# Forget sums of the sampled requests: gathered by key, summed on chip, added to the scores by a product with the unit matrix

## The chip, the cores and the metric

The program runs on one core of one Trainium2 chip. The metric is the device time of one execution in microseconds (us), from the first to the last work of the core. The core has TensorE (PE, with weight loads shown as PEld), VectorE (DVE), ScalarE (ACT), GpSimd (POOL) and SyncE (SP), which here does nothing but issue DMAs. All data is fp32 unless bf16 is named.

## The reference

Two decoder layers handle one new sequence of 1024 positions and, with the same weights, eight sampled requests of eight new tokens each, whose 2048 past positions lie in pages of 128. One of four mixers is attention with forget gates (FoX). For a request it computes:

```
suf  = reversed cumsum of past_logf  -  past_logf      # per head: the sum over all later past positions
lnew = cumsum(logf)                                    # over the eight new tokens
fk   = concat([-suf, lnew])
score[t, key] = q[t] . k[key]  +  lnew[t] - fk[key]    # masked beyond the token, then softmax
```

So each score of a past key gets two terms: `suf` of its key (2048 keys, 4 heads, 8 requests) and `lnew` of its query row. The page table says in which pages of the cache the request's keys and log forget values lie.

## The kernel before

**Stages of a layer.** The first stage normalises, makes the GLU product and then, tile by tile, the input projections; beside it POOL gathers the NSA cache in 16 pieces of 1 MB (`raw_in`, line 2377) and the sampled requests' compressed keys are made. A barrier (`everyone`, `arrive`) ends it. The attention stage follows (about 474 to 1000 us in layer 0, 2454 to 2985 in layer 1), then merge and the feed-forward products (`gemm`, line 884), which the change does not touch.

**The attention stage.** Its order is written out by hand: 96 units `u` (4 heads, 8 tiles of queries, 3 kinds). Per unit PE makes the scores of unit u+2 (`scores`, line 1220), transposes the probabilities of unit u (line 1253), then does the extras of the unit, then the values of u-1 (`values`, line 1239). DVE takes the row maximum (`row_max`, line 1973), ACT the exponential (line 1489). The work of the eight requests is cut into extras (`extras_of`, `request_steps`): request b begins at unit 7 + 10 b. `kt` transposes its keys (line 1121), `ds` makes its scores (line 1128 for the FoX keys, s below 4, with strips of 32 columns; line 1138 for the NSA keys), `pt` transposes its probabilities, `pv` makes its values. All extras and the transposes of the probabilities share two PSUM banks in turn: `open_group` waits until DVE or ACT has emptied the group before last. In FoX `ds`, DVE adds the tile BIAS to the scores as it copies them out and takes their maximum (`scored`, line 2071).

**How BIAS comes about.** At the start of the attention stage POOL gathers the log forget values, one page a partition (LFP, line 2404). DVE scans each head (line 1914) and copies the totals; PE multiplies them by a triangular mask that adds the totals of later pages (line 1196); DVE makes `suf` (`later_sums`, line 1926, suf_ready). SP stores it to suf_s in eight DMAs (line 696), copies it within DRAM into bias_s, once per new token (line 699, 2 MB), and loads it for each request (`bias_in`, line 717). The terms of new keys go by new_s (line 679) and sixteen copies (line 692); the query terms come into FQ by sixteen small loads (line 688). POOL adds FQ and a mask to BIAS (lines 2429 and 2431, bias_add).

**Queues.** SP's queue in the attention stage, in order: KV4, `head_in(0)` (lines 669 to 672: QN, QF, KF, VF of a head), GH, new_s, the q_in loads (680 to 683), GB and FQ, the copies to bias_s, the stores of suf_s, the copy of line 699, `sparse_in(0)` (sixteen page loads at line 707, each with the page number read from a table, and four more), `bias_in(0)`, two outputs, `head_in(1)`, then per unit: at unit 9 the rank exchange (lines 738 to 746), at unit 12 + 10 b `bias_in(b+1)`, at unit 7 + 10 b `sparse_in(b)` after `pv` of the request before, and at units 27, 51, 75 the head's output and a further head load. POOL's queue: the forget gather, four memsets (line 2408), a wait for suf_out, the gather `fox_in(1)` (line 2393, 4.2 MB: keys and values of request 1 into KVP[1]; LFP, PFX and SUF lie in the same memory), then BIAS by request, with `fox_in(b)` after `pv(b-2)`. `fox_in(0)` is issued at the end of the first stage. DVE's queue: the scans, the copies of ten groups `kv` and `q`, `later_sums`, `row_max(0)`, `row_max(1)`, then unit by unit. PE starts `q` transposes (line 1022) when all four loads of `head_in(0)` have landed.

Of the kernel before, what the change touches and what calls it, by code (L numbers as in the profile page):

```python
# [46 lines left out]
SUFW = PAST // 4 + NT  # L47
# [12 lines left out]
def shape_constants():  # L60
# [26 lines left out]
    parts["later"] = ((q // NPG == k // NPG) & (q > k))  # L87
# [60 lines left out]
def build_step(nc, A, O, layers=DEPTH, stop=99):  # L148
    ctx = ExitStack()
    with ctx, nc.allow_non_contiguous_dma(reason="columns of a few elements in small tables"):  # L150
# [18 lines left out]
        suf_s = scratch("suf_s", (NB, 4 * NH, PAST // 4))  # L169
        bias_s = scratch("bias_s", (NB * 4 * NH, NT, SUFW))  # L170
        new_s = scratch("new_s", (NH, NB, NT))
# [19 lines left out]
        page_rows = fixed.take(1).bitcast(I32)  # L191
# [13 lines left out]
        t1 = Layout(arena, glu_at, ARENA_W)  # L205
        Z = t1.take(1164)
# [69 lines left out]
        FQ = lo.take(NB)  # L276
        GB = lo.take(NB * 3, b=NB, c=3)
        BIAS = lo.take(SUFW)
# [6 lines left out]
        KNT = lo.take(4 * NS, g=4, n=NS)  # L285

        lo = Layout(arena, lo_end, ARENA_W - 544)
        WNP = lo.take(4 * P, j=4, n=P)
        SF = lo.take(SUFW)
        SSL = lo.take(SUFW)  # L290
# [7 lines left out]
        OO = lo.take(GW, h=NH, d=HD)  # L298
# [6 lines left out]
        l2 = Layout(arena, late_at - (P + NT) - SUFW, late_at)  # L305
# [28 lines left out]
        l2 = Layout(arena, kp_at, kp_at + NPG * 512)  # L334
        LFP = l2.take(PAGE * NH, t=PAGE, h=NH)
        PFX = l2.take(NH * PAGE, h=NH, t=PAGE)
        SUF = LFP.rearrange("p t h -> p (t h)").rearrange("p (g s q) -> p g s q", g=4 * NH, s=4)
        TOT = l2.take(4)
        LAT = l2.take(4)
# [79 lines left out]
        names("lfp_ready page_next tot_ready lat_mm suf_ready suf_out")  # L419
        names("x_out x_in head_in gate_in kv4_in fox_ready sl_in bias_in bias_add snb_in rank_ready rank_out q_in aux_in ocb_in os_out oc_ready sm_ready ce2 dmx dex ee_ready wt_ready vb_ready s_mm nm_ready p_ready pt_T pt_evA pt_evD pv_mm o_done cs_ready ce_ready cp_ready o_ready o_out pad_ready")  # L420
# [3 lines left out]
        names("pool_done2")  # L424
# [107 lines left out]
        def _(sp):  # L532
# [3 lines left out]
            sp.dma_start(page_rows, A["page_table"].rearrange("b j -> (b j)").unsqueeze(1)).then_inc(loaded_once, 16)  # L536
# [21 lines left out]
            with sp.Fori(0, layers) as l:  # L558
# [119 lines left out]
                for h in range(NH):  # L678
                    sp.dma_start(new_s[h], ka_s[SEQ:ROWS, h, HD + 1].rearrange("(b t) -> b t", b=NB)).then_inc(S["old_out"], 16)
# [36 lines left out]
                def bias_in(b):  # L716
                    sp.dma_start(BIAS, bias_s[b * 4 * NH:(b + 1) * 4 * NH].rearrange("g t w -> (g t) w")).then_inc(S["bias_in"], 16)

# [15 lines left out]
                for u in range(NU):  # L734
# [35 lines left out]
                sp.wait_ge(S["old_out"], 16 * (5 * NH + 2))  # L770
# [79 lines left out]
        def _(pe):  # L850
# [6 lines left out]
            pe.wait_ge(loaded_once, 320)  # L857
# [30 lines left out]
            with pe.Fori(0, layers) as l:  # L888
# [177 lines left out]
                def compressed(key):  # L1066
# [3 lines left out]
                    if what == "dk":  # L1070
                        pe.wait_ge(S["q_in"], 64)
                        for n in range(4):
                            last = tr(out[:, n * NS:(n + 1) * NS], KNS[0:NS, n // 2, (n % 2) * P:(n % 2 + 1) * P], ident[0:NS, 0:NS])
                    elif what == "dq":
                        for a in range(2):
                            tr(out[:, a * NS:(a + 1) * NS], QS[0:NS].rearrange("p h d -> p (h d)")[:, a * P:(a + 1) * P], ident[0:NS, 0:NS])
                        for h in range(NH):
                            last = tr(out[0:HD, P + h * NS:P + (h + 1) * NS], QCS[0:NS, h, :], ident[0:NS, 0:NS])
# [148 lines left out]
                def values(u):  # L1227
# [4 lines left out]
                    if u == 8:  # L1232
                        pe.wait_ge(S["suf_ready"], 1)
# [1107 lines left out]
        def _(pool):  # L2341
# [33 lines left out]
            with pool.Fori(0, layers) as l:  # L2375
# [49 lines left out]
                def bias(b):  # L2425
                    if b:
                        pool.wait_ge(S["bias_add"], b)
# [60 lines left out]
```

## Time and profile before

| | us |
|---|---|
| median of 3 runs | 4026.25 (4023.59 to 4027.74) |
| the profiled execution | 4024.69 |
| its span in the trace | 4022.9 |
| PE busy | 3379.5 (84%) |
| PEld busy | 1904.4 (47%) |
| DVE busy | 1439.0 (36%) |
| ACT busy | 979.7 (24%) |
| POOL busy | 178.5 (4%) |

The busy time of PE is that of matmuls; weight loads run beside it. An idle engine in a row is given with what it waited for. A row names the line, the operation, the tile written and the tile read, and how many instructions it merges. fp32 matmuls other than transposes are two instructions each. "DMA to landing" is the time from the issue of a DMA to its semaphore. SPq and POOLq are issuing work of those queues.

### The profile page before, as it was taken

The numbers are of one execution on the slowest core, as the hardware profiler recorded it, in microseconds if no ns is written. First come the engines' busy times: TensorE is split into PE (matmuls) and PEld (weight loads), VectorE is DVE, ScalarE is ACT, GpSimd is POOL, SyncE is SP. The second block draws the span as 40 slices with busy tenths as digits, with TensorE's granted clock in tenths as the row PEclk, the third lists the DMA queues.
The fourth block names the chain that finished last, engine by engine and source line by source line (L and its number), as shares of the span: only waits on it lengthen the run. The fifth ranks groups of instructions, "written<-read, shape, count | busy, mean of one in ns | idle before, by whom it ended". The sixth has DMA issues, their size and how long they took to land.

```text
span 4022.9 us, 55991 instructions
## 1 busy us (share of the span) xinstructions
PE 3379.5 (84%) x22238; PEld 1904.4 (47%) x22454; DVE 1439.0 (36%) x2646; ACT 979.7 (24%) x1745; POOL 178.5 (4%) x136
## 2 busy tenths in 40 slices
PE   6999668888277999899989995788862989998998
PEld 3455356666133444444445553566641444444444
DVE  2566433334433321232127654233336133212311
ACT  2122134444212220121012212344423032102301
POOL 0111100000000000000001111000000000000000
PEclk8999789999688999999989997899985999999999
DMA  6332433430311121111062325233220112102211
GB/s 203 100 101 91 114 118 113 132 117 23 104 34 32 47 58 31 42 52 52 21 199 71 104 85 157 90 130 130 77 92 28 29 47 57 52 10 57 68 42 44
DMA packets 401501, 317.19 MB, mean 79 GB/s; under 512 B 150205, under 2 KB 383322, under 8 KB 393946
## 3 DMA queue, kind: packets, MB, share of 16 engines
q1 hardware_dynamic: 394250, 213.65, 19.2%
q0 software_dynamic: 7072, 101.19, 6.8%
q8 instruction: 108, 1.77, 0.2%
q14 instruction: 71, 0.58, 0.0%
HBM read 272.27 MB, written 51.84 MB: 81 GB/s over the span
## 4 chain that ended last, share of the span: by engine, by line
PE 76%; issue 6%; SPq 6%; DVE 4%; ACT 4%; DMA 3%; POOL 0%; POOLq 0%; DVEq 0%; ACTq 0%
PE PS L884 40%; PE PS L974 12%; PE PS L1239 4%; PE PS L1220 4%; PE PS L902 3%; PE PS L1121 2%; PE PS L876 2%; PE PS L964 2%; SPq L707 1%; PE PS L1162 1%; PE PS L1253 1%; DVE arena L1968 1%; ACT arena L1480 1%; ACT arena L1501 1%; SPq L702 1%
## 5 line engine op out<-in xcount | busy, mean ns | idle before, releaser
L884 PE MATMUL PS<-arena 128*128 128x512 bf16 (+1 forms) x10152 | 1619.1, 318 | 89.5 <-DVE arena L1703 41.7
L884 PEld LDWEIGHTS PS<-arena 128*128 128x128 bf16 x10368 | 789.3, 98 | 918.8 <-issue 91.8
L974 PE MATMUL PS<-arena 128*128 128x512 f32 (+3 forms) x1152 | 483.8, 575 | 0.9 <-ACT arena L1398 0.9
L1374 ACT ACTIVATE arena<-arena 128x1024 bf16<-128x1024 f32 (+1 forms) x112 | 145.7, 1303 | 1267.4 <-PE PS L884 1154.1
L2272 DVE TENSOR_TENSOR arena<-PS,arena 128x1088 f32 (+1 forms) x48 | 62.1, 1293 | 776.5 <-PE PS L884 776.5
L974 PEld LDWEIGHTS PS<-arena 128*128 128x128 f32 (+1 forms) x1152 | 208.9, 185 | 241.0 <-issue 206.5
L1973 DVE TENSOR_REDUCE arena<-PS 128x1 f32<-128x1024 f32 (+5 forms) x192 | 138.9, 724 | 369.6 <-PE PS L1223 369.5
L1220 PE MATMUL PS<-arena 128*128 128x512 f32 (+3 forms) x576 | 228.7, 503 | 5.7 <-ACT arena L1489 4.4
L2305 DVE SCALAR_TENSOR_TENSOR arena<-PS,arena 128x1088 f32<-128x1088 f32 x64 | 82.8, 1293 | 388.8 <-PE PS L884 388.8
L1239 PE MATMUL PS<-arena 128*128 128x64 f32 x1632 | 213.0, 276 | 0.0
L1239 PEld LDWEIGHTS PS<-arena 128*128 128x128 f32 x1632 | 200.8, 194 | 8.1 <-issue 5.0
L1703 DVE TENSOR_TENSOR arena<-arena 128x1024 bf16<-128x1024 f32 (+1 forms) x112 | 170.6, 1525 | 49.1 <-ACT arena L1374 49.1
L1420 ACT ACTIVATE arena<-PS,arena 128x512 f32<-128x512 f32 (+6 forms) x144 | 74.3, 585 | 434.7 <-DVEq L1851 240.7
L1762 DVE SCALAR_TENSOR_TENSOR arena<-arena 128x1024 f32<-128x1024 f32 x240 | 172.3, 782 | 1.1
L1121 PE MATMUL PS<-arena 128*128 128x128 f32 x832 | 136.0, 289 | 39.9 <-DVE arena L1968 20.5
L1501 ACT ACTIVATE arena<-PS 128x512 f32<-128x512 f32 x208 | 124.1, 601 | 182.3 <-PE PS L1121 181.2
L1480 ACT ACTIVATE arena<-PS 128x512 f32<-128x512 f32 (+3 forms) x164 | 78.0, 476 | 347.6 <-PE PS L1253 347.1
L1253 PE MATMUL PS<-arena 128*128 128x128 f32 x816 | 126.7, 280 | 39.7 <-DVE arena L2071 36.9
L1489 ACT ACTIVATE arena<-PS,arena 128x1024 f32<-128x1024 f32 (+5 forms) x192 | 136.1, 709 | 25.0 <-DVE arena L1973 22.6
L902 PE MATMUL PS<-arena 128*128 128x512 f32 (+1 forms) x384 | 133.4, 503 | 8.6 <-DVE arena L1734 8.6
L1121 PEld LDWEIGHTS PS<-arena 128*128 128x128 f32 x832 | 91.9, 144 | 80.9 <-DVE arena L1968 30.6
L1274 PE MATMUL PS<-arena 128*128 128x512 f32 (+1 forms) x72 | 36.8, 681 | 109.6 <-DMA arena<-in_gnorm_g 58.9
(311 smaller groups left out, 2792.9 us busy)
## 6 DMA issues: line engine op xcount, KB each, us to landing
arena<-in_w_ff SPq DMA_DIRECT2D x64, 512.0 KB, 4.1
arena<-in_w_ff SPq DMA_DIRECT2D x32, 1024.0 KB, 5.6
arena<-in_cache_nsa_kv SPq DMA_DIRECT2D x256, 64.0 KB
x_s<-arena SPq DMA_DIRECT2D x2, 4352.0 KB, 19.2
arena<-x_s SPq DMA_DIRECT2D x2, 4352.0 KB, 13.1
arena<-in_w_in SPq DMA_DIRECT2D x4, 2048.0 KB, 11.5
arena<-in_w_out SPq DMA_DIRECT2D x16, 512.0 KB, 4.2
arena<-o_s SPq DMA_DIRECT2D x48, 128.0 KB, 2.4
```

What stands on the lines that cost most here:

```text
L884: last = mm(PS[:, 1536 * k + a:1536 * k + a + wd], ww[:, c, :], xx[:, c, a:a + wd], start=c == 0 and n == 0, stop=c == blocks - 1 and n == 2)
L902: last = mm(PS[:, 1536 * s + a:1536 * s + a + n], Wg[:, k, (2 * s + f) * P:(2 * s + f + 1) * P], XNT[:, k, a:a + n], start=k == 0, stop=k ...
L974: last = mm(PS[0:r, c * 512:c * 512 + b - a], XNT[:, j, t * P:t * P + r], Wt[:, j, a:b], start=j == 0, stop=j == KD - 1)
L1121: last = tr(out[:, j * P:(j + 1) * P], src, ident)
L1220: last = mm(PS[:, at:at + len(part) * P], q[:, i * P:(i + 1) * P], kt[:, part[0] * P:(part[-1] + 1) * P], start=True, stop=not masks)
L1239: last = mm(PS[:, at:at + HD], PTR[u % 2][:, n * P:(n + 1) * P], v, start=n == 0, stop=n == len(js) - 1)
L1253: last = tr(out[:, (j - a) * P:(j - a + 1) * P], PR[u % 2][:, j * P:(j + 1) * P], ident)
L1374: run(WH[k][:, 0:blocks, :], WF[k][:, 0:blocks, :], ACT.Copy).then_inc(S["w_hi"], 1)
L1501: run(dst, src, ACT.Copy).then_inc(S["pt_evA"], 1)
L1703: V.tensor_tensor(WL[k][:, 0:blocks, :], WF[k][:, 0:blocks, :], WH[k][:, 0:blocks, :], ALU.subtract)\
L1762: last = V.scalar_tensor_tensor(y, x, CWT[:, c, j:j + 1], y, ALU.mult, ALU.add)
L1973: V.reduce_max(NMX[k][:, v:v + 1], PS[:, (u % 2) * 1024:(u % 2) * 1024 + P * len(keys_of(u))], AX, negate=True).then_inc(S["nm_ready"], 1)
```

## The change

Everything that went by suf_s, bias_s and new_s is gone, and BIAS with it. The log forget values are gathered in key order, sixteen consecutive positions a partition and eight gathers a layer (LF2), into memory of the first stage, after the GLU product. DVE scans them per head with a restart at each request; PE adds the totals of later partitions; `later_sums` is one addition (LAT). POOL forms SUFX for one request at a time: LAT minus the running sum, widened over the tokens. In FoX `ds` PE adds SUFX, taken as the weights, times the unit matrix into the same PSUM group; the new keys' term FKL comes in the same way, once a request. The query term FQ is made by one product in `dq` and is added by DVE in place of BIAS. `fox_in(1)` follows the memsets. DVE makes FQL and FKL (`gates_of_new`) after `later_sums` and ahead of `row_max(0)`.

```diff
@@ SyncE @@
-            sp.dma_start(page_rows, A["page_table"].rearrange("b j -> (b j)").unsqueeze(1)).then_inc(loaded_once, 16)
...
-                for h in range(NH):
-                    sp.dma_start(new_s[h], ka_s[SEQ:ROWS, h, HD + 1].rearrange("(b t) -> b t", b=NB)).then_inc(S["old_out"], 16)
...
+                sp.dma_start(FQ8[0:NS], qa_s[SEQ:ROWS, :, HD]).then_inc(S["q_in"], 16)
+                sp.dma_start(FK8[0:NS], ka_s[SEQ:ROWS, :, HD + 1]).then_inc(S["q_in"], 16)
...
-                    for c in range(4):
-                        r = 32 * c + h * NT
-                        sp.dma_start(FQ[r:r + NT, :], qa_s[SEQ:ROWS, h, HD].rearrange("(b t) -> t b", t=NT)).then_inc(S["aux_in"], 16)
-                sp.wait_ge(S["old_out"], 16 * NH)
-                for c in range(4):
-                    for h in range(NH):
-                        sp.dma_start(bias_s.rearrange("(b g) t w -> g b t w", b=NB)[4 * c + h, :, :, PAST // 4:],
-                                     new_s[h].unsqueeze(1).to_broadcast([NB, NT, NT])).then_inc(S["old_out"], 16)
-                sp.wait_ge(S["suf_ready"], 1)
-                for b in range(NB):
-                    sp.dma_start(suf_s[b].rearrange("g (s j q) -> j (g s) q", s=4, j=NPG),
-                                 SUF[b * NPG:(b + 1) * NPG].rearrange("p g s q -> p (g s) q")).then_inc(S["suf_out"], 16)
-                sp.wait_ge(S["suf_out"], 16 * NB)
-                sp.dma_start(bias_s[:, :, 0:PAST // 4], suf_s.rearrange("b g w -> (b g) w").unsqueeze(1)
-                             .to_broadcast([NB * 4 * NH, NT, PAST // 4])).then_inc(S["suf_out"], 16)
...
+                sp.wait_ge(S["tot_ready"], 1)
                 sparse_in(0)
-                sp.wait_ge(S["suf_out"], 16 * (NB + 1))
-                sp.wait_ge(S["old_out"], 16 * 5 * NH)
-                bias_in(0)
...
-                    if 0 <= b < NB - 1 and o == 5:
-                        sp.wait_ge(*evacuated(GROUP_AT["ds", b, 3]))
-                        bias_in(b + 1)
@@ TensorE @@
-                        pe.wait_ge(S["q_in"], 64)
+                        pe.wait_ge(S["q_in"], 96)
...
+                        pe.wait_ge(S["fl_ready"], 1)
+                        last = mm(out[:, 384:384 + NB], FQL[0:NS].rearrange("p c h t -> p (c h t)"), C("same_req", NS), start=True, stop=True)
...
+                            if s == 0:
+                                pe.wait_ge(S["suf_ready"], b + 1)
+                            gates = SUFX[:, 4 * s:4 * s + 4].rearrange("p c h t -> p (c h t)")
+                            last = mm(out[:, 0:P], gates, ident, start=False, stop=True)
...
+                                last = mm(out[:, P:P + NT], FKL[0:NS].rearrange("p c h t -> p (c h t)"), ident[0:NS, new], start=False, stop=True)
...
-                mm(bank(7, 4), C("later"), TOT, start=True, stop=True).then_inc(S["lat_mm"], 1)
+                mm(bank(7, NH * NB), C("later"), TOT.rearrange("p h b -> p (h b)"), start=True, stop=True).then_inc(S["lat_mm"], 1)
@@ VectorE @@
-                dve.wait_ge(S["lfp_ready"], 1)
+                dve.wait_ge(lfp_in, 128 * l + 128)
...
+                def gates_of_new():
+
+                    dve.wait_ge(S["q_in"], 96)
+                    wide = [NS, NH, NT]
+                    for c in range(4):
+                        V.tensor_tensor(FQL[0:NS, c], FQ8[0:NS].unsqueeze(2).to_broadcast(wide),
+                                        C("same_tok", NS).unsqueeze(1).to_broadcast(wide), ALU.mult)
+                        last = V.tensor_copy(FKL[0:NS, c], FK8[0:NS].unsqueeze(2).to_broadcast(wide))
+                    last.then_inc(S["fl_ready"], 1)
...
+                            last = scored(SF[:, s * P:(s + 1) * P], out[:, 0:P], FQ[:, b:b + 1].to_broadcast([P, P]), MX[:, 0, s:s + 1])
+                            if s == 3:
+                                last = scored(SF[:, 512:520], out[:, P:P + NT], FQN[:, b, :], MX[:, 0, 4:5])
...
                 later_sums()
+                gates_of_new()
                 row_max(0)
@@ GpSimd @@
+                pool.wait_ge(S["glu_mm"], 2)
+                for b in range(NB):
+                    G.indirect_dma_start(LF2[:, b * NPG:(b + 1) * NPG, :].rearrange("p n h -> p (n h)"), None,
+                                         A["cache_fox_logf"].rearrange("l n (q r) h -> (l n q) (r h)", r=NPG),
+                                         bass.IndirectOffsetOnAxis(block_rows[:, b:b + 1], 0)).then_inc(lfp_in, 16)
...
-                pool.wait_ge(S["suf_out"], 16 * NB)
-
                 pool.wait_ge(S["pad_ready"], 4)
                 fox_in(1)
-                pool.wait_ge(S["aux_in"], 320)
...
+                def later(b):
+
+                    if b:
+                        pool.wait_ge(S["pt_T"], done(("ds", b - 1, 3)))
+                    wide = [P, NPG, NH, NT]
+                    G.tensor_tensor(SUFX, LAT[:, :, b].unsqueeze(1).unsqueeze(3).to_broadcast(wide),
+                                    PFX[:, :, b, :].rearrange("p h r -> p r h").unsqueeze(3).to_broadcast(wide),
+                                    ALU.subtract).then_inc(S["suf_ready"], 1)
+
+                pool.wait_ge(S["lat_ready"], 1)
+                later(0)
                 fox_landed(0)
```

## Rows read from the trace of the kernel before

**Rows 1.** The page's chain that ended last: shares of the span by engine.

```profile
PE 76%; issue 6%; SPq 6%; DVE 4%; ACT 4%; DMA 3%; POOL 0%; POOLq 0%; DVEq 0%; ACTq 0%
```

**Rows 2.** Waits of PE, layer 0's attention: total, times, longest us.

```profile
PE PS L1253 <- DVE arena L2071: 18.8, 1, 18.8
PE PS L1022 <- DMA arena<-va_s: 9.7, 2, 6.7
```

**Rows 3.** The same, start of layer 1's attention.

```profile
PE PS L1253 <- DVE arena L2071: 18.1, 1, 18.1
PE PS L1022 <- DMA arena<-va_s: 3.2, 1, 3.2
```

**Rows 4.** Timeline of PE: start, duration, line, tiles, count, idle before and releaser.

```profile
531.73 0.22 PE L1223 MATMUL PS<-arena 128*128 128x128 bf16 x1
550.76 1.30 PE L1253 MATMUL PS<-arena 128*128 128x128 f32 x5 [18.82 <-DVE arena L2071]
555.06 1.06 PE L1022 MATMUL PS<-arena 128*64 128x128 f32 x4 [3.00 <-DMA arena<-va_s]
```

**Rows 5.** Timeline of SP's queue: copy, pages of request 0, its bias.

```profile
516.46 0.60 SPq L699 DMA_DIRECT2D bias_s<-suf_s  x1
518.77 25.44 SPq L707 DMA_DIRECT2D arena<-in_cache_nsa_kv  x16
545.96 0.35 SPq L717 DMA_DIRECT2D arena<-bias_s  x1
```

**Rows 6.** Timelines of POOL (first two rows) and DVE.

```profile
517.22 1.02 POOL L2393 DMA_INDIRECT arena<-in_cache_fox_kv,arena  x1 [34.18 <-issue]
548.84 1.05 POOL L2429 TENSOR_TENSOR arena<-arena 128x520 f32<-128x520 f32 x1 [30.60 <-DMA arena<-bias_s]
493.59 1.42 DVE L1973 TENSOR_REDUCE arena<-PS 128x1 f32<-128x1024 f32 x2 [1.46 <-PE PS L1223]
550.32 0.29 DVE L2071 CUSTOM_DVE_ANT_0 arena<-PS,arena 128x128 f32<-128x128 f32 x1 [19.30 <-POOL arena L2431]
```

**Rows 7.** Stretches: length, busy by engine (PE to POOL), clock, DMA share, GB/s.

```profile
550.00:554.00 4.00, 1.30 (x5) 0.93 (x5) 1.20 (x4) 0.60 (x1) 0.17 (x1) 0.50 1.30 239
554.00:556.00 2.00, 0.94 (x5) 0.83 (x6) 0.00 (x0) 0.00 (x0) 0.00 (x0) 0.50 0.23 43
556.00:558.00 2.00, 2.00 (x22) 1.26 (x21) 0.00 (x0) 1.19 (x2) 0.00 (x0) 0.50 0.09 5
```

**Rows 8.** Groups by shape, layer 0's attention: count, busy us, mean ns, idle.

```profile
L1239 PE MATMUL PS<-arena 128*128 128x64 f32 x816 | 105.3, 274 | 0.0
L1220 PE MATMUL PS<-arena 128*128 128x128 f32 x72 | 15.4, 296 | 2.2 <-ACT arena L1489 2.2
```

**Rows 9.** Timeline of all engines at the start of layer 0's attention.

```profile
475.61 7.04 POOL L2408 MEMSET arena<- 64x2048 f32 x4
479.29 1.92 SPq L672 DMA_DIRECT2D arena<-va_s  x1
485.74 1.46 PEld L1022 LDWEIGHTS PS<-arena 128*64 128x64 f32 x8 [0.44 <-issue]
```

**Rows 10.** Issue to landing: line 672 (VF), line 2393 (fox_in), line 699 (copy).

```profile
DMA to landing us min/median/max: 4.5/4.8/5.9
DMA to landing us min/median/max: 13.1/14.4/18.7
DMA to landing us min/median/max: 20.8/20.9/20.9
```

**Rows 11.** Issue to landing, line 628: stretch 260 to 345, then 430 to 445.

```profile
DMA to landing us min/median/max: 5.8/5.8/5.8
DMA to landing us min/median/max: 1.8/1.8/1.8
```

**Rows 12.** DMA queues, 445 to 475 (fox_in(0)): packets, MB, share.

```profile
q0 software_dynamic: 144, 4.19, 34.6%
```

**Rows 13.** Timeline of POOL in the first stage.

```profile
164.51 1.18 POOL L2377 DMA_INDIRECT arena<-in_cache_nsa_kv,arena  x1 [56.68 <-PE PS L951]
```

More of the change, by code:

```diff
@@ L85, in shape_constants @@
     parts["btril"] = (same & (k <= q))[:, :NS]
-    parts["later"] = ((q // NPG == k // NPG) & (q > k))
+    parts["later"] = (q > k)
+    parts["within"] = np.broadcast_to(k % NPG != 0, (P, P))
+    eight = np.arange(NT)[None, :]
+    parts["same_tok"] = (r[:, None] % NT == eight)
+    parts["same_req"] = (r[:, None] // NT == eight)
     m = np.arange(NS // 2)[None, :]
@@ L205, in build_step @@
         t1 = Layout(arena, glu_at, ARENA_W)
+        LF2 = t1.take(NB * NPG * NH, n=NB * NPG, h=NH)
         Z = t1.take(1164)
@@ L275, in build_step @@
         QNALL = QS.rearrange("p h d -> p (h d)").rearrange("p (b n) -> p b n", b=NB)
-        FQ = lo.take(NB)
+        FKL = lo.take(P, c=4, h=NH, t=NT)
         GB = lo.take(NB * 3, b=NB, c=3)
-        BIAS = lo.take(SUFW)
+        PFX = lo.take(NH * NB * NPG, h=NH, b=NB, r=NPG)
+        LAT = lo.take(NH * NB, h=NH, b=NB)
+        SUFX = lo.take(4 * P, r=NPG, h=NH, t=NT)
         VN1 = lo.take(384)
@@ L297, in build_step @@
         late_end = lo.at
[L298 removed]
+        OO = QCS
         l2 = Layout(arena, late_at, late_end)
@@ L418, in build_step @@
         names("raw_T raw_ev phi_in pe_in cp_T cp_ev kvc_mm conv_done z_mm z_ev z_free na_ready ex_ready lf_ready small_mm fin st0 st1 tail_T tail_ev tail_out y_out old_out")
-        names("lfp_ready page_next tot_ready lat_mm suf_ready suf_out")
-        names("x_out x_in head_in gate_in kv4_in fox_ready sl_in bias_in bias_add snb_in rank_ready rank_out q_in aux_in ocb_in os_out oc_ready sm_ready ce2 dmx dex ee_ready wt_ready vb_ready s_mm nm_ready p_ready pt_T pt_evA pt_evD pv_mm o_done cs_ready ce_ready cp_ready o_ready o_out pad_ready")
+        names("tot_ready lat_mm lat_ready suf_ready fl_ready")
+        names("x_out x_in head_in gate_in kv4_in fox_ready sl_in snb_in rank_ready rank_out q_in aux_in ocb_in os_out oc_ready sm_ready ce2 dmx dex ee_ready wt_ready vb_ready s_mm nm_ready p_ready pt_T pt_evA pt_evD pv_mm o_done cs_ready ce_ready cp_ready o_ready o_out pad_ready")
         names("oa_hi u_hi oa_in0 oa_in1 ss_ready oa_ready oa_T oa_ev y_in y_sq y_mm y_c")
@@ L1132, in request @@
                                     for c in range(4):
-                                        last = mm(out[32 * c:32 * (c + 1), P:P + NT], QALL[:, a, b, :], KNT[:, a, new],
-                                                  start=a == 0, stop=a == 1)
+                                        mm(out[32 * c:32 * (c + 1), P:P + NT], QALL[:, a, b, :], KNT[:, a, new],
+                                           start=a == 0, stop=False)
+                                last = mm(out[:, P:P + NT], FKL[0:NS].rearrange("p c h t -> p (c h t)"), ident[0:NS, new], start=False, stop=True)
                         else:
@@ L2423, in fox_landed @@
                     pool.sem_inc(S["fox_ready"], 1)
-                def bias(b):
+                def later(b):
                     if b:
-                        pool.wait_ge(S["bias_add"], b)
-                    pool.wait_ge(S["bias_in"], 16 * (b + 1))
-                    G.tensor_tensor(BIAS, BIAS, FQ[:, b:b + 1].to_broadcast([P, SUFW]), ALU.add).then_inc(S["pool_done2"], 1)
-                    pool.wait_ge(S["pool_done2"], b + 1)
-                    G.tensor_tensor(BIAS[:, PAST // 4:], BIAS[:, PAST // 4:], C("newneg"), ALU.add).then_inc(S["bias_add"], 1)
-                fox_landed(0)
-                bias(0)
-                for b in range(2, NB):
-                    bias(b - 1)
-                    fox_landed(b - 1)
-                    pool.wait_ge(S["pt_T"], done(("pv", b - 2)))
-                    fox_in(b)
-                bias(NB - 1)
-                fox_landed(NB - 1)
-                pool.wait_ge(S["bias_add"], NB)
+                        pool.wait_ge(S["pt_T"], done(("ds", b - 1, 3)))
[5 more added lines that the diff above has]
+                later(0)
+                fox_landed(0)
+                for b in range(1, NB):
+                    later(b)
+                    fox_landed(b)
+                    if b < NB - 1:
+                        pool.wait_ge(S["pt_T"], done(("pv", b - 1)))
+                        fox_in(b + 1)
                 G.tensor_scalar(block_rows, block_rows, POOL * (P // NPG), None, ALU.add)
```

74 lines of the change are left out of this document (28 added, 46 removed).

## Prediction

> **What bounds the kernel.** I read the chain of waits first. It lies 76% on TensorE (PE) [rows 1], so an edit counts where PE waits or where PE gets work; SP, POOL and DVE count only through PE. Then the waits of PE in the two attention stages, the only stages that the edit's steps touch (the eight moved gathers apart). In layer 0 the largest wait inside the loop over units is 18.8 us ahead of a line-1253 transpose, put down to DVE's scoring of line 2071, and the transposes of line 1022 wait 9.7 us in two places for head loads, the longer 6.7 [rows 2]. Layer 1 repeats it: 18.1 and, for the first head load, 3.2 [rows 3]. Then the timelines around the wait. PE stops at 532.0 and resumes at 550.76 [rows 4]. DVE's scoring of request 0 waited for bias_add, POOL's additions at 548.84 [rows 6], these for bias_in(0), issued at 545.96, and SP issued that behind the sixteen page loads of sparse_in(0), which took from 518.77 to 544.21 and stood behind the broadcast copy into bias_s at 516.46 [rows 5]. So what ends last is SP's queue: copy, pages, bias. The head load of head_in(1) follows in the same queue, and PE waits 3.00 us more for it at 555.06 [rows 4].
>
> **Part by part. Removed.** (1) The bias wait: 18.8 + 18.1 = 36.9 us [rows 2, 3]. What is late next? DVE works through rank(5) just before its scoring and PE reaches line 1223 at 531.73 [rows 4]; DVE's gap before the scoring is 19.30 us and ends at 550.32 [rows 6], so DVE was free at 531.0, ahead of PE. I take the whole wait as gone. (2) The head_in(1) wait, 3.0 + 3.2 = 6.2: without the 45 small and large DMAs of bias_s, suf_s, new_s and FQ between, the pages (25.4 us, one layer's issue) can start near 490 instead of 518.77 and end by 515, or by 524 if SP is held up as below; the load then lands about 5 later, and PE asks for it near 535 to 542. The rank exchange of unit 9 stands behind the same loads in SP's queue and moves earlier with them. Both waits gone. (3) After the wait PE works at a granted clock of 0.50, the 1.2 GHz level: 1.30 + 0.94 + 2.00 us of work in 550 to 558 [rows 7]; at 2.4 GHz it is half, 2.1 saved per layer, 4.2 together. (4) POOL's additions over BIAS (1.05 us, off the chain) give way to SUFX, of 512 instead of 520 columns: nothing. Sum removed: 36.9 + 6.2 + 4.2 = 47.3.
>
> **Added on PE.** Four products with `ident` for each of eight requests and one for the new keys: 40 a layer, 80 in all, fp32, so two instructions each, with 128 weight columns. They are not in the trace. Below: the 128x64 values products with the same kind of weights are paced at 105.3/816 = 0.129 us an instruction [rows 8], 0.26 a product. Above: scores of 128x128 with their gaps, 15.4/72 = 0.214, so 0.43. I take the low end: the step stands in a run of products, as the values do, and 64 or 128 columns are no longer than the load of 128 weights. 80 x 0.26 = 20.8. About five of them (1.2 us) a layer vanish in the 6.7 us wait for head_in(2) [rows 2], since request 2's products lie between the step that lets SP go and that wait, at least in layer 0, and I take it for both: -2.4. The product in "dq" and the wider `later` product: 0.3 a layer, 0.6. Could a product come free? Not below zero: it is in PE's order and PE has no other wait there. DVE gains one scoring of 8 columns a request, eight small operations of gates_of_new and the FQ copies: within DVE's idle time, 0.5 a layer for the two places where PE is near, 1.0. Sum: 20.8 - 2.4 + 0.6 + 1.0 = 20.0.
>
> The Trainium skill, TensorE: Matmul & The Clock Gate, section LDWEIGHTS, gives a weight load as columns over 1.2 GHz, by which I estimate 0.107 us a load and 0.21 a product; the sum would be 4 us lower, inside my range, and the 0.129 of this trace is used.
>
> **Moved: the gather fox_in(1).** This is what I trust least. Before, POOL may issue it only after suf_out, at 517.22 [rows 6]; now it follows the memsets. These start at 475.61, behind the forget gather, and take 7.04 [rows 9]; without that gather they end near 481, and fox_in(1) goes out near 481.6, its data from about 482.8. At that time the head loads of head 0 are still running: VF is issued at 479.29 and its landing takes 5.9 (the longest of its line), so 485.2 [rows 9, 10], and PE's first transposes of q go at 485.74. Gathers take 13.1 to 18.7 us to land [rows 10]. What does a big gather do to small packets of SP's queue? Stores of 128 KB land in 1.8 us by themselves and in 5.8 with the 1 MB piece gather beside them [rows 11]: they land when it has ended. And the broadcast copy of 2 KB rows took 20.8 beside the second gather's 18.7 [rows 10]: it ended with it, though it has 64 rows on each of 16 engines and the gather 144/16 = 9 packets [rows 12], so the turns are finer than the gather's packets. If the copy's 64 rows just fit, a turn is some 4 KB, 64 turns in about 10.5 us of data; VF has 64 small packets an engine left, with the tail of KF some 76. With one a turn, head_in(0) lands near 495.5: 10 us later. With turns of 2 KB it is near 491: 6 later. I take 8 a layer, 16 in all; the bounds are 0 (fair shares) and 12 (the whole flight).
>
> The Trainium skill, DMA: Bandwidth & Descriptors, section Queues, rings and completion order, speaks against this part too: an engine takes turns between the rows it has work for at packet granularity, and the section SWDGE vs HWDGE vs iDMA puts a software packet at preferably no more than 4096 B. By that rule the later time, 10 a layer, holds; with free sharing by bytes it would be 2. The stores' row agrees with the rule, the packet size is only inferred here.
>
> **Added waits.** On DVE gates_of_new waits for all six q_in loads ahead of row_max(0); behind it stand ACT's first exponential and all PE transposes of the units. row_max(0) starts at 493.59 [rows 6] for PE's scores, so q_in has until about 492, or 500 where the start has slid by 8, and they leave earlier than before (SP has four loads of new_s less ahead of them). I give it nothing beyond the 8. PE's wait for fl_ready stands behind that, its wait for suf_ready far behind POOL's single operation. POOL's later(b) waits for ds(b-1,3), and behind it fox_landed(b), needed only at the next request's kt(0). SP's wait for tot_ready is met at about 476. The eight forget gathers, near 1.0 us each, lie on POOL between raw_in(1) and raw_in(2): there POOL idles 56.68 us until 164.51 for transposes that PE makes after the GLU product [rows 13], so nothing; without that cover it would be 8 us a layer. The page_rows load and its wait: below 1 us, once, left out.
>
> **Sum.** -47.3 + 20.0 + 16 = -11.3 against the profiled execution's 4024.7 (span 4022.9 and 1.8 around it): 4013.4. The median of the three runs is 1.6 above that, 4026.25, so the prediction is 4015.
>
> **Rivals.** (A) The forecast, 0.46: 4015, on its own 4005 to 4023. (B) The gather does not hold the loads up (0 to 2 us a layer): 16 less becomes 2, so 4001, 0.20. For it: the loads are nearly done when it starts. Against it: the stores. (C) The gather takes whole packets of 29 KB (4.19 MB/144) as its turn, so the loads wait for its whole flight, and q_in behind them: 12 a layer, 8 more than A, 4023, 0.12. Against it: the copy ended too soon for that. (D) Slower. The products are not paced by weights in a run but each pays its single duration: a 128x128 fp32 score takes 0.296 an instruction [rows 8], 0.59 a product, for instance as each closes an accumulation behind four strips of 32 columns. 80 x (0.59 - 0.26) = 26 more: 4041. It decides from 0.26 + 11.3/80 = 0.40 a product. Against it: PE's instructions overlap everywhere in the loop. 0.12. (E) The change doesn't do what it says: another wait stands where the bias wait stood (SP's pages or the rank exchange, if SP is held up for the flight and then late), and half of the 37 us stays: 4015 + 18 = 4033, 0.10. The margin of 10 us and more that I find speaks against it.
>
> **How the numbers follow.** About 0.2% (8 us) is what a measurement can tell from no change: below 4018 or above 4034. Faster: 0.40 of A, all of B, a little of C and E: 0.62. Same: the rest of A, most of C and of E: 0.27. Slower: D, nearly all: 0.11. The range takes in B and the edge of E: 3998 to 4034.
>
> **What would show it.** In the profile after: no PE wait for line 2071 at unit 9 and none for va_s at its q transposes; fox_in(1) issued near 482; the landing of VF near 493 (A), 487 (B) or 497 (C); row_max(0) near 502 in layer 0; the new products paced near 0.26, PE busy up by 10 a layer. I would be wrong if the first transposes of q are not late, if the pace is 0.4 or more, or if DVE's row_max(0) waits for q_in rather than for PE.

## The result and the profile after

| | us |
|---|---|
| before, median of 6 runs | 4026.99 (4022.33 to 4029.4) |
| after, median of 6 runs | 3995.41 (3992.05 to 4010.01) |
| ratio, 95% interval | 0.9928 [0.9912, 0.9944] |
| span of the profiled execution, before and after | 4022.9 and 3994.4 |

The change is 31.6 us faster. The forecast was 4015, and the range ended at 3998, so the time lies below it. The page of after, its parts 1 and 4:

```profile
PE 3403.9 (85%) x22618; PEld 1925.2 (48%) x22618; DVE 1446.7 (36%) x2690; ACT 976.9 (24%) x1745; POOL 192.3 (5%) x132
...
PE 77%; DVE 7%; issue 5%; ACT 4%; DMA 3%; SPq 2%; POOL 1%; POOLq 0%; DVEq 0%; ACTq 0%
```

SP's queue went from 6% of the chain [rows 1] to 2%, DVE from 4% to 7%. PE's busy time is 24.4 us above the 3379.5 of before; the difference can't be read to a microsecond, since the trace of before lacks 216 of its matmul records (22238 beside 22454 weight loads) and after's lacks none. To see where time came from I cut both traces at the same events: the issue of KV4, the merge products, the first products of w_out, the first and the last of the feed-forward part.

| us, layer 0 / layer 1 | before | after | difference |
|---|---|---|---|
| attention, KV4 to merge | 508.5 / 512.7 | 508.3 / 499.9 | -0.2 / -12.8 |
| product with w_out | 106.4 / 107.3 | 107.4 / 107.2 | +1.0 / -0.1 |
| feed-forward part (in layer 0 with the next layer's start) | 789.1 / 773.4 | 780.6 / 766.4 | -8.5 / -7.0 |

About half of the gain, 15.5 us, is in the feed-forward part, in which the diff touches no line. There each block of 72 bf16 products ends with an evacuation by DVE. Two blocks in a row of before, then of after (start, duration, engine, line, operation, count, idle before it and its releaser):

```profile
1340.33 1.29 DVE L2305 SCALAR_TENSOR_TENSOR arena<-PS,arena 128x1088 f32<-128x1088 f32 x1 [5.95 <-PE PS L884]
...
1351.52 1.29 DVE L2305 SCALAR_TENSOR_TENSOR arena<-PS,arena 128x1088 f32<-128x1088 f32 x1 [5.94 <-PE PS L884]
```

```profile
1339.77 1.29 DVE L2301 SCALAR_TENSOR_TENSOR arena<-PS,arena 128x1088 f32<-128x1088 f32 x1 [5.83 <-PE PS L864]
...
1350.83 1.29 DVE L2301 SCALAR_TENSOR_TENSOR arena<-PS,arena 128x1088 f32<-128x1088 f32 x1 [5.82 <-PE PS L864]
```

A block takes 11.19 us in before and 11.06 in after, and all 28 distances from 1300 to 1960 us agree within 0.02. The down blocks, of 144 products, take 22.38 and 22.12. The instructions are the same. What differs is their place in memory: before's constants are 3416 words wide and `page_rows` takes one more, after's constants are 3560 words and `page_rows` is gone. So XT and everything laid out behind it begin at byte 4 of a 64-byte line in before and at byte 0 in after, counted from the start of the layout.

In the attention stage the two waits went as forecast. PE's waits in after, 470 to 560 us (total, times, longest), then PE's timeline where unit 9 stood still before [rows 4]:

```profile
...
PE PS L1207 <- ACT arena L1476: 7.6, 1, 7.6
PE PS L1103 <- DVE arena L1959: 1.9, 2, 1.7
PE PS L1002 <- DMA arena<-va_s: 1.6, 1, 1.6
```

```profile
532.00 0.22 PE L1210 MATMUL PS<-arena 128*128 128x128 bf16 x1
532.05 0.50 PE L1240 MATMUL PS<-arena 128*128 128x128 f32 x3
532.39 1.40 PE L1103 MATMUL PS<-arena 128*128 128x128 f32 x8
```

There is no wait for DVE's scoring (line 2066 now) in place of the 18.8 us [rows 2] and none for head_in(1). But a new wait of 7.6 us stands at the start, where before waited 2.2. The timelines of POOL, SP and DVE there, and PE at its end:

```profile
481.92 0.94 POOL L2394 DMA_INDIRECT arena<-in_cache_fox_kv,arena  x1 [0.28 <-POOL arena L2406]
...
486.69 9.05 SPq L688 DMA_DIRECT2D arena<-g_s  x4
497.05 18.13 SPq L695 DMA_DIRECT2D arena<-in_cache_nsa_kv  x16
...
497.63 0.18 DVE L1916 TENSOR_TENSOR arena<-arena 64x32 f32<-64x32 f32 x1 [7.00 <-DMA arena<-ka_s]
...
498.39 1.41 DVE L1964 TENSOR_REDUCE arena<-PS 128x1 f32<-128x1024 f32 x2
...
500.89 0.80 PE L1207 MATMUL PS<-arena 128*128 128x128 f32 x2 [7.56 <-ACT arena L1476]
```

The gather fox_in(1) leaves at 481.92. The q_in loads issued beside it need long. Issue to landing of the qa_s load in before, then in after:

```profile
DMA to landing us min/median/max: 5.1/5.1/5.1
```

```profile
DMA to landing us min/median/max: 13.7/13.7/13.7
```

DVE stands in `gates_of_new` (line 1916) until 497.63 for them, `row_max(0)` behind it starts at 498.39 where it had started at 493.59 [rows 6], then come ACT's exponential and PE.

### The profile page after: what moved, and what is told of

It reads as the page before. It is cut to its first block, busy times and chain, and to the rows that moved or that the text cites. A ratio compares the mean times of both kernels' runs of the same rounds, so it can differ in the third digit from the quotient of the medians.

```text
span 3994.4 us, 56452 instructions
## 1 busy us (share of the span) xinstructions
PE 3403.9 (85%) x22618; PEld 1925.2 (48%) x22618; DVE 1446.7 (36%) x2690; ACT 976.9 (24%) x1745; POOL 192.3 (5%) x132
## 4 chain that ended last, share of the span: by engine, by line
PE 77%; DVE 7%; issue 5%; ACT 4%; DMA 3%; SPq 2%; POOL 1%; POOLq 0%; DVEq 0%; ACTq 0%
PE PS L864 40%; PE PS L954 10%; PE PS L1207 5%; PE PS L1226 4%; PE PS L882 3%; PE PS L1103 2%; PE PS L856 2%; DVE arena L1749 1%; PE PS L1240 1%; PE PS L944 1%; PE PS L1149 1%; DVE arena L1959 1%; ACT arena L1467 1%; PE PS L1110 1%; PE PS L1115 1%
## 5 line engine op out<-in xcount | busy, mean ns | idle before, releaser
L864 PEld LDWEIGHTS PS<-arena 128*128 128x128 bf16 x10368 | 781.0, 99 | 910.2 <-issue 93.4
L1207 PE MATMUL PS<-arena 128*128 128x512 f32 (+3 forms) x576 | 230.3, 507 | 16.3 <-ACT arena L1476 15.1
L1261 PE MATMUL PS<-arena 128*128 128x512 f32 (+1 forms) x72 | 36.9, 680 | 110.5 <-DMA arena<-in_gnorm_g 59.8
## 6 DMA issues: line engine op xcount, KB each, us to landing
x_s<-arena SPq DMA_DIRECT2D x2, 4352.0 KB, 18.1
```

The source lines that it names most:

```text
L864: last = mm(PS[:, 1536 * k + a:1536 * k + a + wd], ww[:, c, :], xx[:, c, a:a + wd], start=c == 0 and n == 0, stop=c == blocks - 1 and n == 2)
L1207: last = mm(PS[:, at:at + len(part) * P], q[:, i * P:(i + 1) * P], kt[:, part[0] * P:(part[-1] + 1) * P], start=True, stop=not masks)
```

## The experiments

My theory after this reading had two halves. The place in memory sets the pace of the bf16 products, and is worth about 18 us. The edit itself is worth about as much as I had forecast, with the start cost going through DVE's wait for q_in. The rival for the first half was that something in the edit (clock, queues, loads of weights) speeds the feed-forward part up. For the second: that the start cost, or the products' cost, is something else.

**The place alone, on the kernel before, and taken away from after.**

```diff
@@ before @@
+        fixed.take(15)
         XT = fixed.take(KD * ROWS, k=KD, n=ROWS)
@@ after @@
+        fixed.take(1)
         XT = fixed.take(KD * ROWS, k=KD, n=ROWS)
```

> The kernel before with 15 unused words ahead of XT, so that XT and every tile behind it begin at a multiple of 64 bytes, as they do in the changed kernel, instead of 4 bytes past one; no instruction differs. Theory 1 (the feed-forward products gained by the address alone): a block of 72 products takes 11.06 us instead of 11.19, the two feed-forward stages gain 15 to 16 us together, the first stage about 2, the time is 4026 - 17 = 4009. Theory 2 (the gain there belongs to something else, as lighter DMA traffic or another state of the clock): the block stays at 11.19 and the time at 4026.

> The changed kernel with one unused word ahead of XT: the tiles begin 4 bytes past a multiple of 64, as in the kernel before. Theory 1: blocks of 11.19 us again, 3995 + 17 = 4012, which is what the edit is worth without the address, against 4015 forecast. Theory 2: blocks stay at 11.06, 3995.

Measured: before with XT and all behind it at byte 0 takes 4003.19 us, ratio 0.9941 [0.9928, 0.9954], with nothing of the edit in it. After at byte 4 takes 4018.69, ratio 0.9982 [0.9973, 0.9991]. The blocks follow the place and not the kernel: 11.06 and 22.13 us in the first, 11.19 and 22.38 in the second, to the hundredth. So the larger part of the 31.6 us is the place: 22.6 us by the first run, 24.5 by the second (31.6 less the 7.1 that it keeps). The edit proper is worth some 7 us, less than the 11.3 of my sum.

**Which operand sees the place.** Only the weights' tiles off, then only the activations' of the up products (XNH and XNL; as OTH and OTL the product with w_out reads them too), with the down products' activations UH and UL left in place as a control within the same run.

```diff
@@ weights by 4 bytes @@
+        lo.take(1)
         WF = [lo.take(16 * P, k=16, n=P) for _ in range(2)]
         WH = [lo.take(16 * P, BF16, k=16, n=P) for _ in range(2)]
         WL = [lo.take(16 * P, BF16, k=16, n=P) for _ in range(2)]
+        lo.take(15)
@@ activations by 4 bytes @@
+        lo.take(1)
         OTH = lo.take(KD * ROWS, BF16, k=KD, n=ROWS)
         OTL = lo.take(KD * ROWS, BF16, k=KD, n=ROWS)
+        lo.take(15)
```

> After, with one word free ahead of the weight tiles of the output and FFN products and fifteen behind them: only their fp32 and bf16 weights (WF, WH, WL) begin at byte 4 of a 64-byte line; the activations (XNH, XNL, UH, UL) and XT stay at byte 0. The 72 products of a block take 11.19 us in before and 11.06 in after. If the weight load sees the address, a block goes back to 11.19 us and the two FFN stages to 789 and 775 (after 780.6 and 766.4), the whole near 4010. If only the moving operand sees it, blocks stay at 11.06 us and the time at 3995.

> After, with one word free ahead of the bf16 activations of the up products (XNH, XNL, which the output products read as OTH, OTL) and fifteen behind them: they alone begin at byte 4 of a 64-byte line; UH and UL, which the down products read, and all weights stay at byte 0. If the moving operand sees the address, the up blocks take 11.19 us in place of 11.06 and the down blocks of twice the size stay at 22.12 us beside them; the FFN stages end halfway, some 784 and 771. If the weights see it, nothing changes: 11.06 and 22.12.

Measured: weights off, 11.06 and 22.12 us, 3998.13. Activations off, 4004.37, and the two kinds of blocks part. DVE's evacuations in that run, up blocks, then down blocks:

```profile
1334.73 1.29 DVE L2303 SCALAR_TENSOR_TENSOR arena<-PS,arena 128x1088 f32<-128x1088 f32 x1 [5.96 <-PE PS L866]
...
1345.92 1.29 DVE L2303 SCALAR_TENSOR_TENSOR arena<-PS,arena 128x1088 f32<-128x1088 f32 x1 [5.94 <-PE PS L866]
...
1609.85 1.29 DVE L2270 TENSOR_TENSOR arena<-PS,arena 128x1088 f32<-128x1088 f32 x1 [17.88 <-PE PS L866]
1631.97 1.29 DVE L2270 TENSOR_TENSOR arena<-PS,arena 128x1088 f32<-128x1088 f32 x1 [20.83 <-PE PS L866]
```

11.19 us for up, 22.12 for down. It is the moving operand, the activations; the weights don't see it. A layer has 32 up blocks, 16 down blocks and 8 of w_out: 32 x 0.13 + 16 x 0.26 + 8 x 0.13 = 9.36 us, 18.7 in both. Before at byte 0 had gained 22.6 beside the 4025.8 of before in its job; its interval, 18 to 29, takes 18.7 in. Whether the few us above 18.7 hang on the place too is open.

The kept traces also say which of the three products of a group (512, 512 and 64 columns) pays. Medians from start to start between 1300 and 1470 us, in before and in after: from the first product to the second 215 and 217 ns, from the second to the third 218.5 and 216, from the third to the next group 32 and 28. So the second and above all the one of 64 columns pay, and the first doesn't.

**The grain.** The same edit with 8, 4 and 2 words ahead (8, 12 and 14 behind).

> As the run with the bf16 activations of the up products moved by one word, but by eight words (32 bytes of 64). With one word the up blocks took 11.19 us, the down blocks stayed at 22.12. If what counts is the 64-byte line, the up blocks take 11.19 us here too; if it is a grain of 32 bytes or less, they take 11.06 us.

> The same by four words (16 bytes). 11.19 us for a grain of 32 or 64 bytes, 11.06 us for one of 16 bytes or less; the down blocks stay at 22.12 us in any case.

> As the runs with the bf16 activations of the up products moved by 4, 16 and 32 bytes, but by 8 bytes. 4 bytes gave 11.19 us a block, 16 and 32 bytes 11.06. If the grain is 16 bytes, 11.19 us here; if it is 8, 11.06. The down blocks stay at 22.12 us.

| moved by | up block | down block (not moved) | time, one run each in three jobs |
|---|---|---|---|
| 0 bytes (after) | 11.06 | 22.12 | 3995.4 (median of 6) |
| 4 | 11.19 | 22.12 | 4004.4 |
| 8 | 11.19 | 22.12 | 4006.6 |
| 16 | 11.06 | 22.12 | 3991.9 |
| 32 | 11.06 | 22.12 | 3990.7 |

The grain is 16 bytes, not the line of 64 that I had named at first. The blocks show it; the times are of single runs, and before itself took 4026.0 to 4031.5 in their jobs. 12 bytes was not tried.

**The moved gather.** POOL holds fox_in(1) until the q_in loads have landed.

```diff
                 pool.wait_ge(S["pad_ready"], 4)
+                pool.wait_ge(S["q_in"], 96)
                 fox_in(1)
```

> The changed kernel, POOL waits for all six q_in loads before it issues fox_in(1). Theory (the gather holds up the small loads): q_in lands about 6 us after its issue instead of 12 to 14, the wait of 7.6 us ahead of line 1207 falls back to 2.2 and the clock comes up earlier; 8 to 10 us a layer, 3977 in all. Rival (the loads are late by their own number, two more of 256 four-byte pieces): the landing stays near 12 us and the time near 3995.

Measured: 3982.42, ratio 0.99 [0.9885, 0.9914], 13.0 below after. The two were timed in different jobs; each taken against before in its own job, they gained 43.3 and 31.6, so holding the gather gave 11.8. The profile says why: PE's wait is back at 2.2 us, and SP gets to its pages at 488.27, not 497.05.

```profile
PE PS L1207 <- ACT arena L1476: 2.2, 1, 2.2
```

```profile
485.51 1.55 SPq L688 DMA_DIRECT2D arena<-g_s  x4
488.27 11.14 SPq L695 DMA_DIRECT2D arena<-in_cache_nsa_kv  x10
```

The gather now lands beside the pages, and PE has no new wait for it. Is DVE's wait the way by which it cost? The next run leaves the gather where after has it and moves only DVE's work; one more does both.

```diff
                 later_sums()
-                gates_of_new()
                 row_max(0)
                 row_max(1)
+                gates_of_new()
```

> After, with the gates of the new rows worked out after row_max(1) in place of before row_max(0), and the gather left where it was put: the q_in loads still land 12 to 14 us after issue, but row_max(0) no longer stands behind them on DVE. If the start cost of 10.4 and 9.2 us a layer goes through this wait of DVE (7.00 us at 497.63), the 7.6 us of line 1207 fall to about 2 and most of the 13 us that holding the gather gave come back: 3984. If it goes through other late loads (head_in(0), new keys, pages from 497 to 515), the wait only moves to the exponentials of unit 0 or to the keys of PE, and the time stays near 3994.

> After, with the index gather of fox_in(1) held until the q_in loads have landed, and the gates of the new rows worked out after row_max(1) in place of before row_max(0). The first alone gave 3982.4. The wait of 2.22 us of line 1207 that it left is for products of PE and ACT, so the second edit should add little: DVE waits for ka_s and its kin until 491 to 492 and row_max(0) could begin up to 2 us earlier, 0 to 2 us a layer. 3980. If the gates' wait was the whole start cost, holding the gather adds nothing to it and this run equals the gates alone.

Measured: gates late alone 3988.5, ratio 0.9891 [0.9875, 0.9908]; both 3985.37, ratio 0.9886 [0.987, 0.9903]. With the gates late PE's start comes at 497.00, 20.0 us after KV4, where after has 26.4 (500.89 less 474.47), although the loads are as late as in after (DVE waits 4.30 us for them, now behind `row_max(1)`):

```profile
497.00 0.80 PE L1207 MATMUL PS<-arena 128*128 128x128 f32 x2 [2.22 <-ACT arena L1476]
```

```profile
500.21 0.18 DVE L1916 TENSOR_TENSOR arena<-arena 64x32 f32<-64x32 f32 x1 [4.30 <-DMA arena<-ka_s]
```

So most of the start cost went through this one wait: 4.9 of 5.8 us a layer by the first column of the table of two pieces below, 9.9 us in all against before of its job. Doing both adds nothing that can be measured to holding the gather, as expected of the theory. (3985.37 is 5 us above the 3980 expected, but before was 4.2 us slower in that job too.) By their ratios, 0.99, 0.9891 and 0.9886, the three versions can't be told apart; each beats after.

**The products.** After without them, and the same with the gather held.

```diff
-                                    mm(out[32 * c:32 * (c + 1), 0:P], QALL[:, a, b, :], KTF[s % 2][:, a, c * P:(c + 1) * P],
-                                       start=a == 0, stop=False)
+                                    last = mm(out[32 * c:32 * (c + 1), 0:P], QALL[:, a, b, :], KTF[s % 2][:, a, c * P:(c + 1) * P],
+                                              start=a == 0, stop=a == 1)
...
-                            gates = SUFX[:, 4 * s:4 * s + 4].rearrange("p c h t -> p (c h t)")
-                            last = mm(out[:, 0:P], gates, ident, start=False, stop=True)
...
-                                last = mm(out[:, P:P + NT], FKL[0:NS].rearrange("p c h t -> p (c h t)"), ident[0:NS, new], start=False, stop=True)
```

> The changed kernel without the 40 products a layer with SUFX and FKL (it leaves the forget terms of the keys out of the sampled requests' scores). If a product costs its pace of 0.26 us: 80 x 0.26 less about 2 absorbed, 3995 - 18 = 3977. If each costs its single duration, 0.6: 3995 - 45 = 3950. If they hide in PE's gaps: 3995.

> After, without the products of the key forget terms and with the gather of fox_in(1) held until the q_in loads have landed (it leaves out the sums of the keys' forget gates in the sampled requests' scores). Alone these gave 3975.6 and 3982.4 beside 3995.4, that is 19.9 and 13.0 us. If the two costs are of separate places (the start of the attention, and one product in each score group), they add up: 3962.5. If the product's cost lies partly in the slow clock after the start, which the held gather removes as well, less than the sum is gained: 3967. Attention by the trace then some 489 and 489 us a layer (after 508.3 and 499.9).

Measured: 3975.55, 19.9 below after; with the gather held 3967.23, 15.2 below the run with the gather held. Against before of each job these are 18.6 and 15.5. The two costs don't quite add up: 27.2 together, 30.4 as a sum. The attention of 494.7 and 488.4 us in the last run's trace was forecast at 489. That the missing part lies in the slow clock after the start, as one of the two expectations has it, these runs don't show: single executions differ by more than the missing 3.2 us in this stage, below.

**The attention stage in two pieces.** The first piece runs from the issue of KV4 to the first value product of request 0, the second from there to the merge. In before these three events are at 473.9, 593.13 and 982.4 us.

```profile
593.13 1.93 PE L1162 MATMUL PS<-arena 128*32 128x256 f32 x32 [0.56 <-DVE arena L1968]
```

```profile
581.47 1.93 PE L1149 MATMUL PS<-arena 128*32 128x256 f32 x32 [0.56 <-DVE arena L1959]
```

```profile
573.58 1.93 PE L1146 MATMUL PS<-arena 128*32 128x256 f32 x32 [0.56 <-DVE arena L1956]
```

These are before, after, and the run without products and with the gather held. In full:

| layer 0 / layer 1, us | start to first value product | from there to the merge |
|---|---|---|
| before | 119.2 / 118.9 | 389.3 / 393.8 |
| before, at byte 0 | 119.1 / 118.2 | 391.7 / 391.5 |
| after | 107.0 / 105.8 | 401.3 / 394.1 |
| after, at byte 4 | 107.7 / 107.3 | 401.5 / 398.5 |
| after, activations moved by 32 bytes | 107.0 / 105.9 | 396.4 / 394.1 |
| after, activations moved by 16 bytes | 104.2 / 104.2 | 398.2 / 398.4 |
| gates late | 101.5 / 101.5 | 400.8 / 397.7 |
| gather held | 100.7 / 100.4 | 398.4 / 397.9 |
| gather held, gates late | 100.5 / 100.6 | 397.9 / 396.1 |
| no products | 106.1 / 102.7 | 393.0 / 389.2 |
| no products, gather held | 99.0 / 99.2 | 395.7 / 389.2 |

The first column is the steadier one, but it too is good to some 3 us only: in the seven kernels that start as after does (after and those with tiles moved) it runs from 104.2 to 107.7, mean of 14 values 106.3. The kernels moved by 16 and 32 bytes differ in no instruction, and in layer 0 PE goes on behind its wait for the first exponential at 502.34 and 502.12, the same 26.3 us after KV4. The stretch from 510 to 520 us, first with 16 and then with 32 bytes, shows what does differ, the granted clock:

```profile
510.00:520.00 10.00, 8.21 (x77) 7.04 (x77) 4.51 (x13) 3.45 (x10) 0.00 (x0) 0.99 0.28 80
```

```profile
510.00:520.00 10.00, 9.06 (x52) 7.16 (x51) 3.28 (x10) 2.30 (x6) 0.00 (x0) 0.50 0.25 73
```

Why it differs no run shows. The second column spreads by 7 us between kernels that are alike in it: 394.1 to 401.5 for the ten with the products, mean of 20 values 398.0; for the four without them (the two kernels of before and the two runs without products) 389.2 to 395.7, mean of 8 values 391.7.

## Why the prediction was wrong, point by point

**The step that failed** is the one that left everything but the attention stages at the time of before ("the only stages that the edit's steps touch"). The widths in the diff's own list of constants and the removed `page_rows` move every later tile by 12 bytes modulo 16, and 18.7 us come from that by the blocks (22.6 and 24.5 by the two whole runs). No rival held it, and no end of the range. The diff showed the edit and the trace the pace of 11.19 us, but neither shows that the pace hangs on the address; a neighbouring run was needed.

**The forecast for the edit proper.** After at byte 4 is the kernel that I had costed: 4018.69 against 4015, ratio 0.9982. It holds within the forecast's own range, but its terms were each too large, and the errors partly cancelled; that the sum came near is in part luck. (The small operations, 1.6 us of my sum, are still there in the runs without products, so they stand in the first line here.)

| us, both layers | forecast | by the two pieces |
|---|---|---|
| waits and slow clock removed, small operations added | -45.7 | -39.9 |
| products | +18.4 | +15.5 |
| start, moved gather | +16 | +11.7 |
| sum | -11.3 | -12.7 |

The right column: 119.05 - 99.1 = 19.95 a layer; 100.55 - 99.1 + 398.0 - 391.7 = 7.75; 106.4 - 100.55 = 5.85. Its sum leans on means over several kernels, and 12.7 lies outside the direct comparison: after at byte 4 with before says 7 us, with an interval of 4 to 11. With the 18.7 of the address the right column gives 31.4, where 31.6 were measured, but 7.1 and 24.5 give the same sum. How the remaining 6 us divide between edit and address is not settled.

- **Bias wait and head_in(1) wait.** Both are gone and nothing took their place, as forecast; rival E falls. What was too large is the 36.9 us of the bias wait. SP's queue set the end of that wait, so its length depends on when PE arrives, and I had read it from one execution. Stretches of before (length, busy by engine, granted clock, DMA share, GB/s), then of before at byte 0, which has the same instructions, with the end of its wait, then of the run without products and with the gather held:

```profile
500.00:510.00 10.00, 8.92 (x63) 5.91 (x62) 5.67 (x22) 2.31 (x6) 0.00 (x0) 0.81 0.14 10
510.00:520.00 10.00, 8.99 (x66) 6.91 (x64) 6.39 (x16) 4.03 (x12) 1.02 (x1) 1.00 0.43 57
...
550.00:560.00 10.00, 6.24 (x41) 4.59 (x42) 2.65 (x10) 2.98 (x6) 0.17 (x1) 0.58 0.61 108
```

```profile
500.00:510.00 10.00, 9.13 (x35) 6.42 (x34) 3.44 (x14) 1.74 (x4) 0.00 (x0) 0.50 0.14 10
510.00:520.00 10.00, 9.86 (x70) 8.08 (x70) 5.34 (x15) 3.13 (x10) 1.02 (x1) 0.77 0.54 88
```

```profile
535.24 0.22 PE L1224 MATMUL PS<-arena 128*128 128x128 bf16 x1
550.56 1.30 PE L1254 MATMUL PS<-arena 128*128 128x128 f32 x5 [15.11 <-DVE arena L2072]
```

```profile
500.00:510.00 10.00, 9.06 (x35) 6.58 (x33) 3.83 (x16) 1.74 (x4) 0.00 (x0) 0.50 0.46 148
510.00:520.00 10.00, 9.82 (x72) 7.86 (x71) 5.45 (x15) 3.13 (x10) 0.00 (x0) 0.81 0.76 162
```

  In before at byte 0 the clock is 0.50 and 0.77 from 500 to 520, where before has 0.81 and 1.00. PE reaches the last product ahead of the wait at 535.24 instead of 531.73, waits 15.1 us instead of 18.8, and goes on at 550.56 instead of 550.76: the slow clock costs that kernel nothing, because the wait takes it up. In layer 1 the wait is 15.2 against 18.1. With the wait gone nothing takes it up, and the run without products has the same slow stretch, 0.50 and 0.81. Had I sized the waits by this second execution, 15.1 + 15.2 + 3.1 + 3.2, with the 4.2 for the slow work behind the wait and the 1.6 of small operations, the line would read -39.2, where -39.9 was found. So the slow stretch at 550 went away with the wait, as forecast, and the one at 500 was there without the edit. What brings it about in one execution and not in another, no run shows; none changed the clock alone.
- **Products.** The pace was taken as 0.26 us a product, 20.8 for 80. Taking them out gave 18.6 and 15.5 against before of each job, and 15.5 by the pieces, 0.19 to 0.23 a product. Rival D (0.59 each, 4041) falls. With the gather held PE is busy for 3388.0 us with them and 3363.4 without, 12.3 a layer, where 10 was forecast. In the timeline of after the next work starts 0.32 us behind a product:

```profile
539.49 0.49 PE L1115 MATMUL PS<-arena 128*128 128x128 f32 x2
539.81 0.60 PE L1103 MATMUL PS<-arena 128*128 128x128 f32 x4
```

  That would be 25.6 us for 80, so part of it seems to lie under waits that PE has anyway; no run shows under which.
- **The moved gather.** fox_in(1) left at 481.92, as forecast (near 482). The size, 8 a layer, was near the 5.9 found, the way was wrong. The head loads, for which I had reckoned the delay, were hardly held: PE's first transposes waited 1.6 us for va_s (1.4 with the gather held) and began at 485.19, so one of my signs of being wrong came true. That was rival B's condition, and its 4001 lies nearest to the 3995.41, but by luck: the start cost that it left out was there, by the other way, and the address made up for it. The six q_in loads were held, and I had written that I would be wrong if `row_max(0)` waited for them and not for PE; it does, 7.00 us at 497.63. The working gave DVE's wait for q_in "nothing beyond the 8", and so missed that it can be taken away by itself, with two lines. `row_max(0)` came at 498.39, neither near 502 nor where before had it.
- **Turns between queues.** The Trainium skill (DMA: Bandwidth & Descriptors) has an engine take turns between rows at packet granularity (section Queues, rings and completion order) and puts a packet at preferably no more than 4096 B (section SWDGE vs HWDGE vs iDMA). From that came my estimate of 10 a layer for the delay of the head loads. The trace shows the small q_in loads, issued just behind the gather, landing in 13.7 to 12.2 us, and in 3.6 to 2.3 with the gather held: 10 us each, the size that the estimate gave. The turns themselves no run shows. For VF, issued 2.1 us ahead of the gather, the estimate gave too much: 0.2 us by PE's waits.

## What to carry to other kernels

When a change alters the width of anything in a hand-made memory layout, work out the byte offset of every later tile modulo 16, and count the moved bf16 operands as touched; better, round each tile to 16 bytes, and compare kernels at the same offsets. A wait for small loads doesn't belong ahead of the first work of a stage when a large gather has just been started: either hold the gather or take the loads' consumer out of the way, which gave back 11.7 and 9.8 us of 11.7 by the pieces. A wait whose end another queue sets is worth what PE has left of it, and a slower stretch ahead of it eats it up: read its length in more than one execution before taking it as the gain. Time a run against the old kernel in the same job. Where a sum's terms come with opposite signs, each should be tested alone, since a total that fits can hide three misses.

## What the runs showed of the hardware

- bf16 products with 512, 512 and 64 moving columns run 1.2% slower where the moving operand begins 4 or 8 bytes past a multiple of 16: 11.19 against 11.06 us for 72, or 1.8 ns a product. Weights at such an address cost nothing (11.06). The 64-column product pays most: 32 against 28 ns to the next start. fp32 was not tried by itself: in the first stage the starts of fp32 instructions with 512 moving columns are 429 ns apart (median) in before and in after, and the stage ahead of the attention, whose large products are fp32 and whose tiles moved alike, took 420.9 and 422.2 us in before, 420.8 and 420.1 in after.
- Small loads issued just behind a gather of 4.2 MB land when the gather does or shortly after (the gather 13.8 us after its issue): 12.2 to 13.7 us in after, 2.3 to 3.6 with the gather held until they are in.
- The same instructions can meet another granted clock. In before the stretch from 500 to 510 us has 0.81, in before at byte 0 it has 0.50, with 63 and 35 matmul instructions in it. Ahead of the bias wait that cost nothing (18.8 us of wait became 15.1, its end stayed at 550.8 and 550.6); in a stage without such a wait the first piece took 107.0 us with 0.50 from 510 to 520 and 104.2 with 0.99.
